# Hybrid RWKV7 / SSD / PEER block: the 32x32 triangular inverses of the recurrence by forward substitution on GpSimd, through DRAM, in place of TensorE's doubling levels

## The reference, cut to what matters

```python
def step(state, inp):
    r_t, w_t, k_t, v_t, kk_t, kka_t = inp
    sa = jnp.einsum('bhvk,bhk->bhv', state, kk_t)
    state = state * w_t[:, :, None, :] - sa[..., None] * kka_t[:, :, None, :] + v_t[..., None] * k_t[:, :, None, :]
    return state, jnp.einsum('bhvk,bhk->bhv', state, r_t)
```

## Time and profile before

| | us |
|---|---|
| median of 3 runs (4180.76 to 4182.44) | 4181.46 |
| span of the profiled execution, first to last instruction | 4168.4 |
| turn 0 of the recurrence | 76.7 |
| turns 1 to 14, mean of one | 85.6 |
| TensorE busy in one turn of 85.08 | 84.4 |
| VectorE busy in the same turn | 48.1 |
| ScalarE busy in the same turn | 24.1 |
| GpSimd busy in the same turn | 5.3 |

### The profile page before, as it was taken

The page is one execution under the profiler, slowest core; times in us unless marked ns, Lnnn a source line. Parts: engine busy times, 40 slices in busy tenths (PEclk is TensorE's granted clock), DMA queues, the critical chain, the costliest instruction groups (busy, mean ns, idle before and its releaser), DMA issues. The chain is left out here.

```text
span 4168.4 us, 80943 instructions
## 1 busy us (share of the span) xinstructions
PE 3753.8 (90%) x35591; PEld 2292.0 (55%) x35591; DVE 2050.6 (49%) x3418; ACT 717.9 (17%) x1304; POOL 783.5 (19%) x755
## 2 busy tenths in 40 slices
PE   7999999999999989999999999989977777777776
PEld 3466666666666655666668888656422223222222
DVE  1355565555555546777772000036454554554544
ACT  2223222322223212122121000010110100100101
POOL 3000000001000000001000000004544444444532
PEclk9999999999999999999999999999999999999998
DMA  9211111111111116665564444429999999999997
GB/s 382 92 36 49 47 49 38 44 42 47 50 37 49 36 30 229 189 210 161 183 192 159 155 162 163 188 84 419 402 405 427 404 408 427 406 407 427 406 427 309
DMA packets 394620, 872.98 MB, mean 209 GB/s; under 512 B 16684, under 2 KB 234430, under 8 KB 325054
## 3 DMA queue, kind: packets, MB, share of 16 engines
q0 software_dynamic: 73728, 536.90, 30.8%
q1 hardware_dynamic: 228864, 284.82, 19.9%
q10 hardware_dynamic: 91710, 46.43, 3.9%
HBM read 863.87 MB, written 4.23 MB: 208 GB/s over the span
## 5 line engine op out<-in xcount | busy, mean ns | idle before, releaser
L2571 PE MATMUL ps<-w_slots,diag 128*128 128x512 f32 x1920 | 899.9, 615 | 286.5 <-DMA w_slots<-in_peer_v,ixv 252.4
L2571 PEld LDWEIGHTS ps<-w_slots,diag 128*128 128x128 f32 x1920 | 356.9, 195 | 827.5 <-issue 507.4
L979 PE MATMUL ps<-hT,w_slots 128*128 128x512 f32 (+1 forms) x1536 | 630.5, 538 | 3.1 <-PEq L230 2.2
L1719 PE MATMUL ps<-hT,w_slots 128*128 128x256 f32 (+1 forms) x1504 | 500.1, 486 | 6.5 <-PEq L655 4.9
L2348 DVE SCALAR_TENSOR_TENSOR junk<-w_slots,hT 128x2048 f32<-128x2048 f32 x128 | 293.4, 2292 | 291.6 <-DMA w_slots<-in_peer_u,ixu 288.5
L2348 DVE SCALAR_TENSOR_TENSOR junk<-ybT,hT 128x2048 f32<-128x2048 f32 x128 | 293.4, 2292 | 273.6 <-DMA ybT<-in_peer_u,ixu 271.8
L2238 POOL DMA_INDIRECT w_slots<-in_peer_v,ixv x244 | 291.4, 1194 | 499.7 <-PE ps L2571 465.1
L1719 PEld LDWEIGHTS ps<-hT,w_slots 128*128 128x128 f32 x1504 | 281.6, 190 | 173.3 <-issue 152.7
L979 PEld LDWEIGHTS ps<-hT,w_slots 128*128 128x128 f32 x1536 | 267.5, 190 | 177.6 <-issue 153.9
L2441 ACT ACTIVATE diag<-ident,coef 128x128 f32<-128x128 f32 x240 | 94.6, 400 | 934.7 <-PE ps L2571 924.9
L695 POOL TENSOR_TENSOR bonus<-Kh 128x256 f32<-128x256 f32 x16 | 11.8, 735 | 1175.4 <-DVE Kh L916 1175.4
(11 more groups left out here) (393 smaller groups left out, 4752.7 us busy)
## 6 DMA issues: line engine op xcount, KB each, us to landing
w_slots<-in_w_mod SPq DMA_DIRECT2D x128, 512.0 KB, 4.8
w_slots<-in_w_in SPq DMA_DIRECT2D x56, 1024.0 KB, 5.6
w_slots<-in_w_in ACTq DMA_DIRECT2D x44, 1024.0 KB, 6.7
w_mod_ring<-in_w_mod SPq DMA_DIRECT2D x16, 2048.0 KB, 13.6
w_slots<-in_w_in SPq DMA_DIRECT2D x7, 4096.0 KB, 13.7
w_slots<-in_w_branch_a SPq DMA_DIRECT2D x4, 4096.0 KB, 13.4
w_slots<-in_w_branch_b SPq DMA_DIRECT2D x4, 4096.0 KB, 13.6
w_slots<-in_w_out SPq DMA_DIRECT2D x4, 4096.0 KB, 12.8
```

The lines of the kernel that those rows point to most:

```text
L979: last = mm(ps[:, 4, t0:TOK], w[m % 2][:, k, :], hT[:, k, t0:TOK], start=(k == 0), stop=(k == KC - 1))
L1719: last = mm(out, w[m % SLOTS_W][:, k, :], hT[:, k, t0:TOK], start=(k == 0), stop=(k == KC - 1))
L2571: last = nc.tensor.matmul(ps[:, 4 * n + c, :], diag[:, k % 2, :], vb[k % NB][:, c * 512:(c + 1) * 512], start=False, stop=False)
```

## The change

The four levels, their start and their evacuations go. In their place the masked triangular blocks are written to DRAM, read back so that each of the 128 partitions holds one 32x32 system (each system twice, once for the even and once for the odd columns of the inverse), and GpSimd runs forward substitution over 31 rows with two instructions a row, an outer product and a subtraction. The result goes to DRAM and from there to where `solved` reads it. VectorE transposes the blocks of one direction before (`St`) and after (`Yt` to `XTp`). Banks 0 to 3 are free of levels, so transposes and `old_right` move there; `bv` of direction d lies in bank 2 + d. TensorE's stream is rewritten around this, and so are the other streams.

```diff
+                    if B:
+                        blocks = lambda m: m.rearrange("p h (n t) -> p (h n) t", t=CH)
+                        for d, name in ((0, "gs0"), (1, "st")):
+                            sp.wait_ge(*VB.by(name, i))
+                            sp.dma_start(s_dram[d].rearrange("j r s t -> (r s) j t"), blocks(AB[:, 0, 0:2, :] if d == 0 else St[:, :, :])).then_inc(s_out, 16)
+                        sp.wait_ge(s_out, 32 * (i + 1))
+                        for e in range(2):
+                            sp.dma_start(Sm[e * HEAD:(e + 1) * HEAD, :, :].rearrange("m s t -> m (s t)"),
+                                         s_dram.rearrange("d j r s t -> (d j r) (s t)")).then_inc(s_in, 16)
...
+                    if B:
+                        sp.wait_ge(*GB.by("solved", i))
...
+                        sp.dma_start(y_dram.rearrange("e d j r k t -> (e d j r) (k t)"), Ym[:, :, :].rearrange("m k t -> m (k t)")).then_inc(y_out, 16)
+                        sp.wait_ge(y_out, 16 * (i + 1))
+                        need(sp, PB, "wu3", i - 1)
+                        need(sp, VB, "xtp", i - 1)
+                        for d in range(2):
+                            for e in range(2):
+                                sp.dma_start(blocks((XTp[e:P:2, 0:2, :], Yt[e:P:2, :, :])[d]),
+                                             y_dram[e, d].rearrange("j r k t -> (r k) j t")).then_inc(y_in, 16)
...
+                def solve_blocks(i):
+                    if i:
+                        pool.wait_ge(y_out, 16 * i)
+                    nc.gpsimd.tensor_copy(Ym[:, :, :], unit[:, :, :]).then_inc(*GB.did("ym"))
+                    pool.wait_ge(*GB.by("ym", i))
+                    pool.wait_ge(s_in, 32 * (i + 1))
+                    for u in range(CH - 1):
+                        n, c = u // 2 + 1, CH - 1 - u
+                        done = SOLVE * i + 2 * u
+                        if u:
+                            pool.wait_ge(solve, done)
+                        nc.gpsimd.tensor_tensor(part[:, 0:n, 0:c], Ym[:, 0:n, u:u + 1].broadcast_to([P, n, c]),
+                                                Sm[:, u:u + 1, u + 1:CH].broadcast_to([P, n, c]), ALU.mult).then_inc(solve, 1)
+                        pool.wait_ge(solve, done + 1)
+                        nc.gpsimd.tensor_tensor(Ym[:, 0:n, u + 1:CH], Ym[:, 0:n, u + 1:CH], part[:, 0:n, 0:c],
+                                                ALU.subtract).then_inc(*((solve, 1) if u < CH - 2 else GB.did("solved")))
...
+                    if 0 <= i < PAIRS:
+                        solve_blocks(i)
...
                 def outputs(n, z, i):
                     if n == 0:
                         pe.wait_ge(*VD.by(f"c{NC - 2}_1", z))
-                        need(pe, VB, "F41", i)
+                        need(pe, AB_, "bv1", i)
...
                 def solved(d, i):
                     if d == 0:
+                        pe.wait_ge(y_in, 64 * (i + 1))
                         pe.wait_ge(*VB.by("xtp", i))
                         pe.wait_ge(*AB_.by("bv1", i))
...
+                    if B:
+                        dve.wait_ge(y_in, 64 * (i + 1))
+                        need(dve, PB, "wu3", i - 1)
+                        nc.vector.transpose(flat(XTp[:, 2:4, :]), flat(Yt[:, :, :])).then_inc(*VB.did("xtp"))
...
+                    piece("v", 0, 4)
                     if B:
                         solved(0, i)
                         solved(1, i)
-                    piece("r", 12, 14)
-                    piece("r", 14, KC)
+                    piece("v", 4, 6)
```

More of the change, by code:

```diff
@@ L178, in front @@
           per_pair, shifts, tanh_w, low_a, gate_g, masks, first_weights, flat_slots):
-    pad_rw, em, ln_eps, off, strict, incl, neg2, id32, id64 = masks
+    pad_rw, em, ln_eps, strict, incl, unit, id64 = masks
     with ExitStack() as stage:
@@ L630, in rwkv @@
         QS = [(d, h) for d in range(2) for h in range(2)]
-        LEVELS = range(1, 5)
         STEPS = range(1, NC - 1)
@@ L888, in _ @@
-                    if A:
+                        shift(1, i, 0, v_s[:, :])
+                        dve.wait_ge(*PA.by("bonus", i))
+                        dve.wait_ge(*VA.by("sh1b", i))
+                        tt(bonus[:, i % 3, :], ps[:, 7, 0:SEQ], v_s[:, SEQ:TOK], ALU.mult).then_inc(*VA.did("bv"))
+                    for j in range(2, NC - 2):
+                        chain(j, z)
+                    if A:
+                        shift(0, p, 0, k_s[:, :])
+                    chain(NC - 2, z)
@@ new lines, in _ @@
+                    if A:
+                        need(dve, PB, "kt1", p - 1)
+                        for d in range(2):
+                            dve.wait_ge(*AA.by(f"rate{d}", p))
+                            nc.vector.tensor_scalar(Kh[:, d, :], Ah[:, d, :], pcol("k_a", p), pcol("om_ka", p), ALU.mult, ALU.add).then_inc(*VA.did(f"kdf{d}"))
+                            dve.wait_ge(*VA.by(f"kdf{d}", p))
+                            dve.wait_ge(*VA.by("sh0b", p))
+                            tt(Kh[:, d, :], Kh[:, d, :], k_s[:, :], ALU.mult).then_inc(*VA.did(f"kd{d}"))
@@ L1188, in piece @@
                             project(name, p, k0, k1)
-                        elif B and (name, k0) in TILE_AT:
-                            next_tile(*TILE_AT[name, k0])
-                        elif not B and (name, k0) in STEPS_AT:
-                            step_sizes(*STEPS_AT[name, k0])
+                        elif name == "k":
+                            (next_tile if B else step_sizes)(k0, k1)
                     if B:
-                        gram(0, 0, i)
-                        gram(0, 1, i)
+                        for d in range(2):
+                            gram(d, 0, i)
+                            gram(d, 1, i)
                     piece("k", 0, 2)
```

433 lines of the change are left out of this document (152 added, 281 removed).

## The result

The changed kernel takes **4236.20 us** (median of 4 runs, 4231.54 to 4243.51) against 4181.11 (4178.91 to 4182.44) for the kernel before on the same chip: ratio 1.0131, 95% interval 1.0118 to 1.0145. It is slower by 55 us, where 44 us faster was forecast. The profiled execution's span grew from 4168.4 to 4231.5, by 63. The 8 us between 63 and 55 are not a cost of the change: in every run with both figures on record the time lies only 1.7 to 2.0 us above the span (4233.28 against 4231.5 here), so the profile before is of an execution of some 4170 us, one of the shorter ones (all runs of that kernel took 4167.0 to 4189.9).

A forecast was written before the change was run, and what follows sets the result against it. TensorE alone was taken to bound the recurrence: turns 1 to 14 lose 10.9 us and gain 3.6, 1.5 and 2.8, −42; with the other turns −44, forecast 4137 us, range 4085 to 4230.

The forecast's parts named there:

- The levels' worth, 10.9 a turn: Removing the three groups of the levels from TensorE's stream was to save 10.9 us in each turn.
- The solve and its trips, 51.2 on the turn clock: Blocks out and back, 30 us of GpSimd solve, way back and transpose: the inverse was to be there at 51.2 us.
- Rival (b): GpSimd's solve becomes the bound if it takes 40 to 43 us instead of 30; 4250 to 4370 us, chance 0.18.
- the 10 of the forecast: Slack at `solved`: TensorE was to ask for the inverse 10 us after it is there.
- The waits (1) and (2): `outputs` waiting for ScalarE's `bv1`, 3.6 us in turns 1 to 14, and the mean waiting for `yf`, 1.5 us.
- The turn without any new wait is 85.6 − 10.9 = 74.7: TensorE's old turn less the levels, 74.7 us, taken as the base to which new waits are added.
- Three waits: All that was added on TensorE's path: `outputs` 3.6 us, the mean 1.5 us and the clock's fall 2.8 us.
- The clock, (3): TensorE's clock falls behind the wait at `outputs`: 6.8 us at the 1.2 GHz level, costing 2.8 us a turn.
- Rival (a): The clock stays up or falls in few turns, so no 2.8 us a turn; 4095 us, chance 0.17.
- Rival (c): Small unseen waits, from new engine orders or r weights delaying small pieces: 3 us a turn 4180, twice 4220; chance 0.20.
- the 0.6 us that would have sunk the forecast: Sign of error: GpSimd's small instructions in the solve taking over 0.6 us on average.
- the 1.8 that I had charged: Extra solve time on GpSimd, 1.8 us, from some 5 us of VectorE's shift and scale of k beside it.

The follow-up runs named there:

- b4: The kernel before without levels 2 to 4, three quarters of the inverse's doubling levels; 4060.46 us, ratio 0.9708.
- e7: Changed kernel with r weights late, Gram products and additions split, `bv1` and `yf` copied early, two pieces of TensorE's work moved over waits; 4034.28 us, ratio 0.9651.
- e8: Changed kernel with 35 further 128x512 copies on GpSimd ahead of each solve, making it some 24 us longer; 4459.57 us, ratio 1.0672.
- e6: Changed kernel with direction 1's Gram products behind the chain step again and r weights issued behind the blocks' way back; 4184.88 us, ratio 1.0015.
- e3: Changed kernel with ScalarE's copy of `bv1` ahead of the gate copy and the exponentials; 4163.59 us, ratio 0.9961.
- b3: The kernel before, levels kept, with the four Gram groups joined and r weights issued ahead of the output's store; 4242.43 us, ratio 1.0146.

## Why the prediction was wrong, point by point

**The levels' worth, 10.9 a turn: right.** The work of 14 turns above gives 10.8, and b4 7.7 of 8.2 for three quarters. e7 reaches a turn of 75.29 against the 74.7 of the sum, with small waits left in it (over all turns 10.0 us at r's padded copy, 4.2 for VectorE at the first transposes, 7.4 in the Gram products, 5.4 at the second part of `outputs` and 5.2 in the chain).

**The solve and its trips, 51.2 on the turn clock: right.** It starts 2.3 later than forecast and is 1.3 shorter; by the trace the inverse's last blocks land near 51.6, and TensorE asks at 65.3. `solved` waits 3.4 us in turn 0, where 6.8 was forecast (that turn kept its 76.5 us all the same, by a Gram wait of 4.2), and 6.2 in turn 15. Rival (b), the solve as the bound, is wrong, and e8 shows the point from which it would be right: 11 to 14 us more, the 10 of the forecast and what TensorE is late by itself.

**The waits (1) and (2): right in place and size,** 3.5 for 3.6 and 1.2 for 1.5.

**The step that failed is "The turn without any new wait is 85.6 − 10.9 = 74.7" together with "Three waits".** The 74.7 is right, but it belongs to an order of TensorE's stream in which nothing else waits, and the changed kernel's isn't that. I looked for waits on other engines at three places of the new order and took every other piece at its old price. The two Gram halves joined and the additions joined are edits of TensorE's order too, as is the r load's new place on SyncE's queue, ahead of the store of the outputs, and I priced none of them. By the wait rows, a turn:

| term, us a turn | forecast | measured |
|---|---|---|
| turn without new waits | 74.7 | 74.8 (85.6 less the measured 10.8) |
| `outputs` on `bv1` | 3.6 | 3.5 |
| mean on `yf` | 1.5 | 1.2 |
| Gram, issue (56.5 − 12.3)/16 | 0 | 2.8 |
| additions, issue (25.4 − 6.3)/16 | 0 | 1.2 |
| variance on `wysq` 11.1/16 | 0 | 0.7 |
| clock, (225 − 31)/16 x 2.8/6.8 | 2.8 | 5.0 |
| sum | 82.6 | 89.2 (the turns: 89.36) |

**The clock, (3): right in kind and in the price of a low microsecond, half its size.** The price stands: in turns 1 to 14 the changed kernel's work takes 1098.40 − 1030.75 = 67.7 us longer than e7's, and its clock is low for 174.0 − 10.2 = 163.8 us more, 0.41 a low microsecond, as 2.8 for 6.8. One fall a turn was forecast, behind `outputs`. There are two in most turns, the other at the Gram wait, and in some a third at the additions: 37 low stretches between 190 and 1660 us against 5. In turns 1, 8 and 11, where the Gram products wait 0.4 to 2 us, none falls near them; in the other thirteen, with 2.9 to 5.1 us of them in one piece, one does. Rival (a), the clock stays up, is wrong. The Trainium skill (TensorE: Matmul & The Clock Gate, section HAM oscillation — how this bites in real kernels) describes this, a fall paid anew in each pass; the trace agrees, here for two waits in a pass.

**Rival (c) was the case,** and its places were named in part ("r weights that delay the small pieces"): the weights delayed TensorE's instructions; that they delayed the small pieces enough to matter no run shows. Its size, 3 us a turn and twice that at the end, fell short of the 6.9 that the four unforeseen rows above add up to (2.8 + 1.2 + 0.7 + 2.2), and its chance of 0.20 was too low for a change that rewrites four instruction streams.

So the levels' 174 us (16 x 10.9) were gained, and 224 given back: 69 to the two waits that I saw (49.4 + 19.9), 74 to three that I didn't (44 + 19 + 11), and 80 to the clock behind them ((225 − 31) x 2.8/6.8), of which I had charged 42. That is 50 more than was gained; with the 10 us at `solved` in turns 0 and 15 it is 59, where the two traces differ by 63 and the medians by 55. The inverse on GpSimd isn't what costs: e7 keeps the solve as it is and is 145 us faster than the kernel before.

What stays open: why the Gram groups still wait with the weights late and the groups apart in a few turns (7 times, 5.2 us in e6), and how far ahead instructions are fetched. What the additions and the variance cost alone no run shows; their rows in the table are wait times. That queue 8's packets bring TensorE's next instructions is inferred: no record names what a packet holds, but the stops end at one fixed distance behind a packet (1.2 to 1.6 us, all 315), and with the weights late the packets come some 2.4 us earlier and the longest stop shrinks by 2.2.

## What to carry to other kernels

When a change rewrites an engine's order, first write down the turn without waits, then walk through the whole new order for waits, joined groups of small matmuls and moved transfers included, and not only the places that the removed work touched. Hundreds of short matmuls in a row can outrun their own instructions; set wide matmuls between them, and issue large loads where such a row isn't running. To tell such a stop from another, look whether a packet of the instruction queue ended just ahead of its end. A wait repeated in each pass costs its length and, if TensorE's clock falls behind it, more (in e3 some 24 us on 49): put a copy that TensorE waits for ahead of table loads, and a piece of work that depends on nothing over each wait that is left.

## What was unexpected of the hardware

TensorE stopped up to 5.1 us in the middle of a loop of 64x32 and 64x64 matmuls whose operands were all there. The stops are in the Gram products, about once a turn (17 times over 16 pairs); they shrink from 56.5 to 30.7 us when a 1 MB load is moved away, to 28.5 when other matmuls stand between the groups, and to 5.2 with both. In the kernel before, the same two edits in the other direction bring them up from 12.3 to 55.2.

The price of such a stop is more than its length: in b3 the waits grew by 42.9 us and the low clock by 72 us, and the kernel by 61.

Small GpSimd operations kept their forecast price: rows of 1 to 31 elements cost nothing to speak of (377 and 394 ns on average, of the 0.6 us that would have sunk the forecast), so the whole solve is 28.7 us where 0.256 an instruction and 2.16 ns an element gave 28.2. In turn 15, where VectorE has no projections of a next pair to work on, the solve takes 27.1; in the other turns it takes 28.5 to 29.0. So the arithmetic of GpSimd alone came out 1.1 below the forecast, and VectorE beside it costs 1.4 to 1.9, about the 1.8 that I had charged. The same shape early in a solve, and while VectorE works on the shift of k:

```profile
832.57 0.32 POOL L724 TENSOR_TENSOR Ypart<-Ym,Sm 128x78 f32<-128x78 f32 x1
...
851.79 0.67 POOL L724 TENSOR_TENSOR Ypart<-Ym,Sm 128x78 f32<-128x78 f32 x1
```

The chain updates on VectorE, which run all through the solve, leave no mark of that size.
